# Two blocks of attention scores issued behind a weight tile instead of inside it, with their maxima moved behind that tile's result

## What is computed

```python
h = rmsnorm(x, norm_mix)
z = h @ w_in
...
qa = rope_partial(qa.reshape(B, T, A_HEADS, 2, A_DH), pos)
ka = rope_partial(ka.reshape(B, T, A_HEADS, 2, A_DH), pos)
...
s = jnp.einsum('bqhmd,bkhmd->bhmqk', q, k) * (A_DH ** -0.5)
s = jnp.where(mask, s, -jnp.inf)
p = jax.nn.softmax(s, axis=-1)
a = p[:, :, 0] - lam * p[:, :, 1]
o = jnp.einsum('bhqk,bkhe->bqhe', a, v)
```

## Time and profile before

| | |
|---|---|
| median of 3 runs | 1527.92 us (1527.22 to 1530.89) |
| the profiled execution | 1522.66 us |
| its span, first to last instruction | 1520.9 us |
| PE busy | 1459.1 us, 96% of the span |
| DVE busy | 878.1 us, 58% |
| ACT busy | 621.8 us, 41% |
| mean granted TensorE clock | 0.967 of full speed |

### The profile page before, as it was taken

How to read it: one execution, slowest core, us unless ns; L and a number is a source line. 1 busy time by engine, 2 the same in 40 slices (tenths; PEclk the granted TensorE clock), 3 DMA queues, 4 the chain that set the end, 5 groups by cost and what they waited for, 6 DMA issues and landing times.

```text
span 1520.9 us, 24935 instructions
## 1 busy us (share of the span) xinstructions
PE 1459.1 (96%) x9763; PEld 1383.4 (91%) x9763; DVE 878.1 (58%) x1440; ACT 621.8 (41%) x1037; POOL 243.4 (16%) x276
## 2 busy tenths in 40 slices
PE   5899899999999999999989999999999999999997
PEld 4799789998899999999978889989888999999997
DVE  4664646657456656545557366475646565555456
ACT  3343343444544433333443334344336443333343
POOL 0302003030004100012412030210300040000234
PEclk9998999999799999999999899999988999999999
DMA  6468965765154454444433977446542454454433
GB/s 155 104 101 93 104 126 119 109 116 116 62 168 139 138 162 141 151 158 142 144 86 103 133 102 107 110 112 112 117 127 83 142 158 143 141 163 155 150 134 104
DMA packets 195550, 191.25 MB, mean 126 GB/s; under 512 B 9126, under 2 KB 192236, under 8 KB 195468
## 3 DMA queue, kind: packets, MB, share of 16 engines
q1 hardware_dynamic: 192352, 181.76, 50.4%
q0 software_dynamic: 2688, 7.35, 1.2%
q10 hardware_dynamic: 428, 1.03, 0.2%
HBM read 181.45 MB, written 8.65 MB: 125 GB/s over the span
## 4 chain that ended last, share of the span: by engine, by line
PE 84%; DVE 7%; POOL 5%; DMA 2%; issue 1%; ACT 1%; ACTq 0%; DVEq 0%; SPq 0%; POOLq 0%
PE big L1206 23%; PE big L1207 22%; PE big L1208 22%; PE X L1341 2%; POOL E L527 2%; PE X L1387 2%; PE X L1340 2%; DVE w_lo L843 2%; PE X L1323 1%; DMA w_raw<-in_w_in 1%; POOL E L528 1%; PE X L1492 1%; PE X L1216 1%; POOL rot L534 1%; PE X L1304 1%
## 5 line engine op out<-in xcount | busy, mean ns | idle before, releaser
L1206 PE MATMUL big<-x_hi,w_hi 128*128 128x320 f32 x1984 | 645.9, 326 | 18.4 <-DVE x_lo L1097 6.9
L1207 PE MATMUL big<-x_lo,w_hi 128*128 128x320 f32 x1984 | 622.6, 314 | 0.0
L1208 PE MATMUL big<-x_hi,w_lo 128*128 128x320 f32 x1984 | 622.4, 314 | 0.0
L843 DVE TENSOR_TENSOR w_lo<-w_raw,w_hi 128x1024 fp32r<-128x1024 f32 (+1 forms) x330 | 418.4, 1271 | 131.5 <-ACT w_hi L559 130.9
L1206 PEld LDWEIGHTS big<-x_hi,w_hi 128*128 128x128 f32 x1984 | 381.2, 192 | 40.1 <-issue 27.1
L559 ACT CAST w_hi<-w_raw 128x1024 fp32r<-128x1024 f32 x328 | 330.1, 1035 | 179.7 <-PE big L1208 81.4
L1207 PEld LDWEIGHTS big<-x_lo,w_hi 128*128 128x128 f32 x1984 | 382.0, 193 | 3.2 <-issue 1.2
L1208 PEld LDWEIGHTS big<-x_hi,w_lo 128*128 128x128 f32 x1984 | 381.3, 192 | 0.0
L504 POOL TENSOR_TENSOR sqt<-xT 128x320 f32<-128x320 f32 x47 | 48.0, 1021 | 638.3 <-DVE xT L1154 422.6
L1206 PE MATMUL big<-h_hi,w_hi 128*128 128x320 f32 x352 | 109.1, 310 | 0.0
L1208 PE MATMUL big<-h_hi,w_lo 128*128 128x320 f32 x352 | 108.9, 309 | 0.0
(11 more groups left out here) (224 smaller groups left out, 1810.6 us busy)
## 6 DMA issues: line engine op xcount, KB each, us to landing
w_raw<-in_w_in SPq DMA_DIRECT2D x130, 512.0 KB, 7.9
w_raw<-in_w_f SPq DMA_DIRECT2D x120, 512.0 KB, 4.3
w_raw<-in_w_pb SPq DMA_DIRECT2D x16, 512.0 KB, 4.3
w_raw<-in_w_pa SPq DMA_DIRECT2D x16, 512.0 KB, 4.0
w_raw<-in_w_o SPq DMA_DIRECT2D x16, 512.0 KB, 4.0
w_raw<-in_w_ple_gate SPq DMA_DIRECT2D x16, 512.0 KB, 4.6
w_raw<-in_w_f SPq DMA_DIRECT2D x16, 384.0 KB, 3.7
k_raw<-in_cache_k SPq DMA_DIRECT2D x8, 256.0 KB, 8.9
```

The lines of the kernel that those rows point to most:

```text
L843: tt(w_lo[:, t % 4, 0:nk, :], w_raw[:, (t // 2) % 2, 0:nk, (t % 2) * P:(t % 2 + 1) * P], w_hi[:, t % 4, 0:nk, :].bitcast(F32), ALU.subtrac ...
L1206: mm(out, wh, xh[:, k0 + k, :], start=start and k == 0, stop=False)
L1207: mm(out, wh, xl[:, k0 + k, :], start=False, stop=False)
L1208: last = mm(out, wl, xh[:, k0 + k, :], start=False, stop=stop and k == nk - 1)
```

## The change

The scores of head 0 leave tile 7 and are issued behind it, ahead of the wait for the GLA operands. The scores of head 1 leave tile 11 and are issued behind it, ahead of the GLA state products. On DVE, `out_tile` of tiles 7 and 11 now comes before `negmax` and no longer behind it. `scores` is an ordinary function now. Nothing else is different; from L1274 on the changed file's line numbers are two lower, and from L1401 on one lower.

```diff
@@ DVE, loop over tiles
                     if t in (6, 7):
+                        out_tile(vgT[:, t - 6, :], t)
                         if t == 7:
                             negmax(0)
-                        out_tile(vgT[:, t - 6, :], t)
...
                     if t in (10, 11):
                         if t == 10:
                             dve.wait_ge(vg_trans, 2 * v)
-                        else:
+                        out_tile(zr[:, t - 10, :], t)
+                        if t == 11:
                             negmax(1)
-                        out_tile(zr[:, t - 10, :], t)
@@ PE, scores(h)
                     q, k, kc = qr[:, h, :], kr[:, h, :], kcT[:, h, :]
-                    yield
-                    yield
                     if h == 0:
@@ PE, loop over tiles
-                         between={7: scores(0), 11: scores(1), 15: gla_outputs()}.get(t, ()))
+                         between={15: gla_outputs()}.get(t, ()))
...
                     if t == 7:
-
+                        scores(0)
                         pe.wait_ge(gla_qk_ready, v)
                         transposes(X[3], E[:, NL, :]).then_inc(k_trans, 1)
...
                     if t == 11:
+                        scores(1)
                         pe.wait_ge(a_ready, 3 * v)
```

## The result

| | before | after |
|---|---|---|
| median of 4 runs | 1527.57 us (1523.94 to 1530.89) | 1538.57 us (1537.48 to 1541.04) |
| ratio, with its 95% interval | | 1.0075 (1.0048 to 1.0102) |
| the profiled execution | 1522.66 us | 1539.57 us |
| its span | 1520.9 us | 1537.8 us |
| mean granted clock | 0.967 | 0.957 |

The change costs 11.0 us between the medians, 0.7%. The two profiled executions are 16.9 us apart, because that of before is among its fastest. Only they can be split by stage. At half clock an execution spends 2 x (1 - mean clock) of its span: 1520.9 x 0.066 = 100 us before and 1537.8 x 0.086 = 132 us after. Half of the 32 us more is lost, 16 us, about the whole difference: the clock's account leaves little for anything else.

A forecast was written before the change was run, and what follows sets the result against it. PE, busy for 96% of the span, was taken to bound the kernel. Terms of 2.1 - 2.1 = 0.0 us plus 5.8 us for the clock (6.5 - 0.7), on the median 1527.92, gave 1533.7 us, range 1525 to 1542 us.

The forecast's parts named there:

- the side that had 0.59: Whole kernel: slower by over 0.3%, from two to five falls (0.53) or late maps (0.06).
- The wait for `E`, no gain: PE behind tile 7: one wait of 1.9 us replaces 0.43 and 1.22; the transposes start when they did.
- Head 0's maxima, +0.3 us an iteration: DVE: tile 7's `out_tile` delays them 0.48 us; PE waits 0.3 for the GLA sum in seven iterations, +2.1.
- the -0.7 of the clock's term: Behind tile 9: where the clock falls, PE is late for the GLA sum and skips the 0.3 us wait.
- Around tile 11, -0.26 us: PE: undivided tile plus head 1's scores take 5.17 us where it took 5.43; eight times, -2.1 us.
- Head 1's maxima, nothing: DVE: they start 2.3 us later, but 1.4 us of slack remains before PE needs `difference(1)`; no cost.
- the third rival: Behind tile 13: head 1's maxima come later than reckoned, PE waits for `difference(1)` in all eight iterations; 1536 us, chance 0.06.
- The sign named for it: In the changed profile, DVE's wait for the scores of head 1 grows by over 2 us.
- The clock at tile 7, +6.5 us: Behind the 1.9 us wait: one chance in two of a fall in five usual iterations, 2.6 us each.
- The row of 1.88 us: Fifth iteration before: wait for rotated k, then 3.4 us at clock 0.50, costing 1.7 us; nearest in length.
- The rule against it: Skill's rule for PE, avoid only longer idle gaps: a 1.9 us gap is harmless, sum stays at 0.0 us.
- The second rival: Tile 15: two more of eight iterations keep the clock, hardly a fall at tile 7; -8.8 us, 1519, chance 0.07.

The follow-up runs named there:

- e2_head1: Kernel before with only head 1's scores and maxima moved, head 0 left inside tile 7: 1519.86 us, ratio 0.9971.
- e1: Kernel before with only head 0's scores and maxima moved, head 1 left inside tile 11: 1543.73 us, ratio 1.0117.
- s2: Changed kernel with the GLA outputs of tile 15 spread over all eight of its chunks: 1517.05 us, ratio 0.9948.
- t2: Changed kernel with the GLA outputs spread over tiles 14 and 15: 1513.80 us, ratio 0.9901.
- pad4: Kernel before with four more large matmuls (0.6 us) ahead of head 1's scores at tile 11, each iteration: 1536.04 us, ratio 1.0061.
- s1: Kernel before with the GLA outputs of tile 15 spread over all eight of its chunks: 1506.52 us, ratio 0.9881.
- s3: Kernel before with head 1 alone moved and tile 15's GLA outputs spread over its eight chunks: 1511.53 us, ratio 0.9908.
- t1: Kernel before with the GLA outputs spread over tiles 14 and 15: 1508.83 us, ratio 0.9885.
- t3: Kernel before with head 1 alone moved and the GLA outputs spread over tiles 14 and 15: 1505.11 us, ratio 0.9845.
- e3: Changed kernel with twelve throwaway large matmuls in the wait for `E`, except in each layer's first iteration: 1521.88 us, ratio 0.9992.
- s4: Changed kernel with the wait for `E` filled by twelve large matmuls and tile 15's GLA outputs spread over its chunks: 1507.32 us, ratio 0.9914.
- t4: Changed kernel with the wait for `E` filled by twelve large matmuls and GLA outputs spread over tiles 14 and 15: 1496.05 us, ratio 0.9801.

## Why the prediction was right, and where it was too low

The time, 1538.57 us, lies in the range, 4.9 us above the forecast of 1533.7, on the side that had 0.59. That it lies inside is in part luck: the forecast moved the time by 5.8 us, the medians moved by 11.0 and the profiled executions by 16.9, and the range had its room above for more falls at tile 7 and not for what came. (The five falls of the forecast's own range make 1527.92 + 11.5 = 1539.4, not 1539.5.) By its own steps:

- **The wait for `E`, no gain.** Predicted 1.9 us in five iterations, near 17 in all; measured 1.92 to 1.94, 18.2 in all. The difference is the 0.97 us of the first iteration, which comes and goes from run to run. That the wait for the rotated q would go held too.
- **Head 0's maxima, +0.3 us an iteration.** Measured 0.23 from the rows of the seventh iteration, and none where a fall came before, as the -0.7 of the clock's term says.
- **Around tile 11, -0.26 us.** Measured -0.20, and -0.19 in e2_head1.
- **Head 1's maxima, nothing.** They start 1036.66 - 1031.25 = 5.41 us behind tile 11's start, before 1022.18 - 1018.97 = 3.21: 2.2 us later, predicted 2.3. It cost nothing in seven iterations, and in the first of this execution PE waited 1.3 us for the map, as in the third rival: the slack had been read from the seventh iteration, and in the first ACT waits longer for its raw weights. The sign named for it was wrong: DVE's own wait for the scores did not grow, it is 1.12 us after 1.53, because DVE now waits 2.02 us ahead of that for tile 11's result.
- **The clock at tile 7, +6.5 us.** The sum is near and its factors are not. Predicted were half of five falls at 2.6 us; measured four of five at 1.46, 5.8 us. That the two agree is luck. From the transposes to tile 8 it was 4.8 us, not 5 to 6. The price came from the second iteration's long fall, because the work behind it was the same. The row of 1.88 us, with a fall of 3.4 us and 1.7 lost, was the nearest in length of the wait, and it had both the length of the fall and nearly its price. Over all the profiles, waits of 1.9 us in the five usual iterations were followed by a fall in 16 of 20 (after, e1, s2, t2), the waits of 1.2 us in none of 35 (before, e2, pad4, s1, s3, t1, t3), and the filled ones in none of 15 (e3, s4, t4).
- **The rule against it.** By the Trainium skill, "TensorE: Matmul & The Clock Gate", section "Why this matters for your kernels", longer idle gaps between bursts of matmuls are to be avoided, and a gap of 1.9 us would have cost nothing. The traces disagree here: falls came behind gaps of 1.9 us in four of five iterations of the changed kernel and in five of five of e1_head0.
- **The step that failed: tile 15.** The prediction gave it no term in the forecast. The second rival took it as a chance of gain alone, 8.8 us for two more good cases, and set the other side aside with the words that "the shift can as well lose it". That was a price too, of the same size: of before's six iterations that another one follows, four took clearly less than 18.4 us (13.96 twice, 15.56 and 16.99), and one took more (19.93). Losing them, less what that one gained, is +11.7 us between the profiles, more than any term of the sum. The earlier trace rows shows the two levels, but its two slow rows are the last iterations of the layers, which stayed as they were; the iterations that had something to lose or to gain are those of the windows above, and of these it looked at the two best alone.

On the medians, 11.0 us, the split cannot be made: executions of before differ by 7 us and more, and only the profiled one shows its tile 15. What is shown is that moving head 0 brings the loss (e1_head0), that filling the wait takes it back (e3_fill), and that 0.6 us more work four tiles ahead costs more than itself with no fall at tile 7 (pad4). How the wait at tile 7 sets the place of the fall in tile 15, and why the bad case repeats in every iteration, stays open. That with equal iterations each tile 15 begins at the same distance from the last fall is no full answer: the seventh iteration had no fall at tile 7, and its tile 15 took 18.4 us too.

## What to carry to other kernels

A wait that a reorder only gathers into one piece costs no time by its length but may cost the clock behind it; a row of before with a wait of that length, and the clock in windows behind it, gives the price. Where a busy stretch runs at two clock levels for the same instructions, count its loss and its gain as terms of any change upstream, and spread its small matmuls between large ones before tuning tenths of a us. Filling an unavoidable wait of PE with matmuls that are thrown away can pay.

## What had not been expected of the hardware

- The clock falls in stretches where PE is busy all the time: from tile 15 to the next tile, PE is busy for 18.4 of 18.4 us at a mean of 0.72.
- 0.6 us more work, four tiles ahead of such a stretch, cost 9.3 us (6.3 to 12.5) over eight iterations, about twice the 4.7 us added (pad4).
- Once fallen, it can stay low through a mix of small and large matmuls: 23.9 us at 0.50 in s1 and in t1, for work that was done at 1.00 in other iterations (t1) or, at the end of a layer, in 18.5 us in another run (s2). The executions of these kernels spread over 13 to 21 us (s1, t1 and s2, the last from 1510 to 1531); that such falls make the spread is likely but not shown, since one execution of each has a profile.
